# Constant products in the pauses of TensorE, split buffers by table, and an accumulator turned before the last down step

## What is computed

```python
def first_block(x, c, ctx, c_ctx, ...):                 # two layers
    for i in range(DEPTH):
        sh1, sc1, g1, sh2, sc2, g2 = ada(c, ada_w[i], ada_b[i])
        h = rmsnorm(x, norm1_g[i]) * (1 + sc1) + sh1
        out = even_mixer(h, h_ctx, ...) if i == 0 else fourier_mixer(h, w_fourier)
        x = x + g1 * out
        x = x + g2 * swiglu(rmsnorm(x, norm2_g[i]) * (1 + sc2) + sh2, w1, w3, w2)
    return x

def second_block(x, c, ...):                            # one layer
    h = rms_norm(x, g_mix) * (1 + sc1) + sh1
    x = x + gt1 * parallel_mixer(h, ...)                # window attention and RG-LRU, merged
    h = rms_norm(x, g_ffn) * (1 + sc2) + sh2
    x = x + gt2 * moe_ffn(h, ...)                       # 32 experts, 4 for a token
    return rms_norm(x, g_final)
```

## Time and profile before

| | us |
|---|---|
| median of 3 runs | 1897.08 (1891.97 to 1900.2) |
| the profiled execution | 1898.97 |
| its span | 1897.2, mean granted clock 0.941 |
| PE busy | 1692.5 (89%) |
| DVE busy | 878.2 (46%) |
| ACT busy | 441.0 (23%) |
| POOL busy | 363.7 (19%) |
| DMA | 586.61 MB, mean 309 GB/s |

### The profile page before, as it was taken

The page is one execution under the profiler, slowest core; times in us unless marked ns, Lnnn a source line. Parts: engine busy times, 40 slices in busy tenths (PEclk is TensorE's granted clock), DMA queues, the critical chain, the costliest instruction groups (busy, mean ns, idle before and its releaser), DMA issues.

```text
span 1897.2 us, 24286 instructions
## 1 busy us (share of the span) xinstructions
PE 1692.5 (89%) x9444; PEld 1071.0 (56%) x9444; DVE 878.2 (46%) x1175; ACT 441.0 (23%) x679; POOL 363.7 (19%) x119
## 2 busy tenths in 40 slices
PE   6989889999889999786899999999986989799776
PEld 2863579999589999664733444334332433344222
DVE  5767579988549988676321221221121212122012
ACT  3324544443334443454200000000000000000001
POOL 1632035553245553553000000000000000000000
PEclk8998989999999999898799999999998989899988
DMA  8623358886338877443599999999999999999994
GB/s 326 238 88 105 118 211 279 285 282 233 137 141 280 286 277 242 150 178 111 231 403 422 421 422 421 421 422 421 420 421 421 421 421 420 421 415 418 422 421 196
DMA packets 100607, 586.61 MB, mean 309 GB/s; under 512 B 12225, under 2 KB 13505, under 8 KB 45153
## 3 DMA queue, kind: packets, MB, share of 16 engines
q1 hardware_dynamic: 100512, 585.35, 79.1%
HBM read 584.26 MB, written 1.05 MB: 309 GB/s over the span
## 4 chain that ended last, share of the span: by engine, by line
PE 57%; DVE 19%; DMA 16%; issue 4%; SPq 3%; ACT 2%; DVEq 0%; ACTq 0%
PE psum L1032 21%; PE psum L1048 10%; DVE accl L1617 7%; DMA araw<-ada_dram 7%; DMA mraw<-dn_dram 4%; PE psum L611 3%; PE psum L1008 3%; PE psum L612 3%; PE psum L613 3%; SPq L398 2%; DMA mraw<-gu_dram 2%; PE psum L1061 2%; DVE accl L1616 2%; DMA mlast<-gu_dram 1%; DVE work L1672 1%
## 5 line engine op out<-in xcount | busy, mean ns | idle before, releaser
L1552 POOL TENSOR_TENSOR wl<-raw,wh 128x1024 fp32r<-128x1024 f32 (+1 forms) x100 | 353.9, 3549 | 510.5 <-ACT wh L1160 291.1
L1032 PE MATMUL psum<-mraw,xsat 128*64 128x512 f32 (+2 forms) x1648 | 413.6, 640 | 40.0 <-DMA mraw<-gu_dram 26.5
L1032 PEld LDWEIGHTS psum<-mraw,xsat 128*64 128x64 f32 (+2 forms) x1648 | 137.3, 143 | 271.5 <-issue 270.5
L1048 PE MATMUL psum<-mraw,xsat 128*64 128x512 f32 (+2 forms) x848 | 208.1, 636 | 12.7 <-DMA mraw<-dn_dram 9.9
L793 PE MATMUL psum<-ah,wh 128*128 128x256 f32 x704 | 203.8, 289 | 15.6 <-DVE al L1676 11.0
L794 PE MATMUL psum<-al,wh 128*128 128x256 f32 x704 | 201.9, 287 | 0.0
L795 PE MATMUL psum<-ah,wl 128*128 128x256 f32 x704 | 201.7, 287 | 0.0
L611 PE MATMUL psum<-ah,wh 128*128 128x256 f32 (+1 forms) x440 | 136.0, 309 | 32.6 <-DVE al L1676 9.5
L1032 PE MATMUL psum<-mlast,xsat 128*64 128x512 f32 (+2 forms) x400 | 146.3, 653 | 16.6 <-DMA mraw<-gu_dram 16.6
L793 PEld LDWEIGHTS psum<-ah,wh 128*128 128x128 f32 x704 | 137.5, 195 | 17.4 <-issue 11.5
L2190 DVE TENSOR_TENSOR oacc<-psum,oacc 128x512 f32<-128x512 f32 x60 | 38.7, 686 | 222.8 <-PE psum L1061 222.8
(11 more groups left out here) (354 smaller groups left out, 2548.0 us busy)
## 6 DMA issues: line engine op xcount, KB each, us to landing
mraw<-gu_dram SPq DMA_DIRECT2D x206, 1024.0 KB, 20.2
mraw<-dn_dram SPq DMA_DIRECT2D x106, 1024.0 KB, 25.5
araw<-ada_dram SPq DMA_DIRECT2D x128, 512.0 KB, 4.5
mlast<-gu_dram SPq DMA_DIRECT2D x50, 1024.0 KB, 21.4
raw<-ffa_dram SPq DMA_DIRECT2D x44, 1024.0 KB, 7.4
raw<-blk_dram SPq DMA_DIRECT2D x56, 512.0 KB, 3.4
raw<-ffb_dram SPq DMA_DIRECT2D x44, 512.0 KB, 5.6
mlast<-dn_dram SPq DMA_DIRECT2D x22, 1024.0 KB, 26.4
```

What stands on the lines that cost most here:

```text
L1032: last = mm(ps[4 + n][a * w:(a + 1) * w, :], xs[:, k * P + a * w:k * P + (a + 1) * w], slots[slot][:, i * 2 * D + n * 512:i * 2 * D + (n + ...
L1048: last = mm(ps[n][a * w:(a + 1) * w, :], at[:, k * P + a * w:k * P + (a + 1) * w], slots[slot][:, i * D + n * 512:i * D + (n + 1) * 512], ...
L1552: sub = lambda o, a, b: nc.gpsimd.tensor_tensor(o, a, b.bitcast(F32), ALU.subtract)
```

## The change

`keep_clock(n)` makes n constant fp32 products (ones by a constant) into bank 7, at six places: 4 behind the sums of norm 1 and the ada columns, 4 behind the loop columns of norm 2, 7 behind the sums of norm 3, 5 behind the loop columns of norm 4, 12 in front of the wait for the merged activations, 7 behind the sums of norm 5. The split buffer of a block comes from a table (`SPLIT`), and the raw blocks 21 to 36 lie behind the first feed-forward slots (`RAW`), so that those can be loaded while blocks are still running. SP issues blocks 21 to 25 and the first feed-forward loads (`ffn_first`) ahead of `ada` 28 to 47; two of the next three blocks are loaded at the end of `ffn`, and the third (the "shared" one, 27 or 36) behind six `ada` chunks and the last `b` split. ACT splits the first feed-forward slots around the last two blocks of a mixer (`last_blocks`), and the next stage's first three blocks at the end of `ffn`, ahead of the squares of norms 2 and 4. POOL does the same in its order, and three times waits for activations before it goes on with blocks (`s_h`, `s_hl`, `s_mnl`). In the tail `sum_turn()`, the 16 transposes of `oacc`, stands ahead of the last chunk of the last down step, and the output tiles lie in five banks in place of eight.

```diff
@@ -44,7 +44,10 @@
 NB = 56
-NRAW, NSPLIT = 3, 6
+NRAW = 3
+SPLIT = [b % 6 for b in range(B_O)] + [0, 1, 4, 5, 2, 3, 4, 5] * 2 + [0, 1, 4, 5, 2, 3] * 2 + [0, 1] + [4, 3, 5, 2, 0, 1, 5, 2]
+SPLIT_BEFORE = [max([k + 1 for k in range(b) if SPLIT[k] == SPLIT[b]], default=0) for b in range(NB)]
+RAW = [(5120 if B_O + NRAW <= b < B_2 + NRAW else 0) + (b % NRAW) * D for b in range(NB)]
...
@@ -345,8 +348,7 @@
         def out_tile(j):
-            bank = (3, 4, 5, 6, 7, 2, 0, 1)[j]
-            return ps[bank][:, 0:T]
+            return ps[(4, 5, 6, 7, 2)[j % 5]][:, (j // 5) * T:(j // 5 + 1) * T]
...
@@ -387,7 +389,7 @@
                     sp.wait_ge(s_lo, b - NRAW + 1)
-                sp.dma_start(raw[:, (b % NRAW) * D:(b % NRAW + 1) * D], blk_d[b]).then_inc(s_raw[b % NRAW], 16)
+                sp.dma_start(raw[:, RAW[b]:RAW[b] + D], blk_d[b]).then_inc(s_raw[b % NRAW], 16)
...
@@ -425,15 +427,11 @@
             ada(25)
-            for b in range(B_O + NRAW, B_O + NSPLIT):
-                blk(b)
...
             ada(27)
-            for b in range(B_O + NSPLIT, B_F):
+            sp.wait_ge(s_v, 4)
+            for b in range(B_O + NRAW, B_F):
                 blk(b)
-            for n in range(28, 48):
-                ada(n)
...
@@ -441,13 +439,21 @@
+            def ffn_first(l):
+                if l == 0:
+                    sp.wait_ge(s_lo, B_O + 2)
+                else:
+                    sp.wait_ge(s_flo, NF)
+                    sp.wait_ge(s_fblo, NF)
+                ffn_a(l, 0, ffna_d[l, 0])
+                ffn_b(l, 0, ffnb_d[l, 0])
+                if l == 0:
+                    sp.wait_ge(s_lo, B_O + NRAW)
+                ffn_a(l, 1, ffna_d[l, 1])
             def ffn(l):
-                sp.wait_ge(s_lo, B_F if l == 0 else B_2)
-                if l == 0:
-                    sp.wait_ge(s_v, 4)
-                for f in range(2):
-                    ffn_a(l, f, ffna_d[l, f])
-                    ffn_b(l, f, ffnb_d[l, f])
+                sp.wait_ge(s_lo, B_F - 1 if l == 0 else B_2)
+                ffn_b(l, 1, ffnb_d[l, 1])
...
@@ -464,24 +470,32 @@
                         ffn_b(l, u % 2, ffnb_d[l, bass.ds(f, 1), :, :].rearrange("a p n -> p (a n)"))
+                shared = B_F + 1 if l == 0 else B_2 + 2
+                for b in range(shared - 1, shared + 2) if l == 0 else range(B_2, B_2 + NRAW):
+                    if b != shared:
+                        blk(b)
...
                     ada(base_n + 40 + j)
+                sp.wait_ge(s_fblo, (l + 1) * NF)
+                blk(shared)
...
                     sp.dma_start(tabs[:, :, :, :], tab_d).then_inc(s_par, 16)
-                else:
-                    sp.wait_ge(s_flo, 2 * NF)
-                    sp.wait_ge(s_fblo, 2 * NF)
-                    for b in range(B_2, B_2 + NRAW):
-                        blk(b)
...
+            ffn_first(0)
+            for n in range(28, 48):
+                ada(n)
             ffn(0)
-            for b in range(B_F, B_2):
+            for b in range(B_F + NRAW, B_2 - 2):
+                blk(b)
+            ffn_first(1)
+            for b in range(B_2 - 2, B_2):
...
             ffn(1)
+            sp.wait_ge(s_flo, 2 * NF)
...
@@ -506,7 +520,7 @@
                 expert_load(i)
-            sp.wait_ge(s_blk, NB - 3)
+            sp.wait_ge(s_blk, NB - 6)
...
@@ -599,10 +613,14 @@
+            def keep_clock(n):
+                for _ in range(n):
+                    mm(ps[7][:, 0:T], ones, con[:, 0:T], start=True, stop=True)
...
                 wait(pe, s_ev, b - 1)
-                w0 = (b % NSPLIT) * D
+                w0 = SPLIT[b] * D
...
@@ -820,12 +838,14 @@
             ada_columns(5)
+            keep_clock(4)
...
             loop_columns(0)
+            keep_clock(4)
...
@@ -851,12 +871,14 @@
             norm_sums(3)
+            keep_clock(7)
...
             loop_columns(1)
+            keep_clock(5)
...
@@ -931,12 +953,14 @@
                 last.then_inc(s_msum, 1)
+            keep_clock(12)
...
             norm_sums(5)
+            keep_clock(7)
...
@@ -988,6 +1012,12 @@
+            def sum_turn():
+                for j in range(DJ):
+                    for t in range(TT):
+                        mm(out_tile(j)[:, t * P:(t + 1) * P], oacc[:, t, j * P:(j + 1) * P], ident,
+                           start=(j < 5 and t == 0), stop=False, is_transpose=True, skip_group_check=True)
...
@@ -1113,6 +1143,11 @@
                                 slots_turn(u + 1)
+                            if c == DN_CH - 1 and u == NU and p_ == 0:
+                                pe.wait_ge(m["added"], 2 * (NU - 1))
+                                pe.wait_ge(m["at"], 2 * NU)
+                                pe.wait_ge(m["gu_read"], 2 * NU)
+                                sum_turn()
...
@@ -1128,17 +1163,13 @@
                 pe.wait_ge(s_pick, PASSES + 1)
+                sum_turn()
...
-            pe.wait_ge(m["added"], 2 * (NU - 1))
-            pe.wait_ge(m["at"], 2 * NU)
+            pe.wait_ge(s_last, 2)
             for j in range(DJ):
-                if j == 6:
-                    pe.wait_ge(s_last, 2)
-                for t in range(TT):
-                    mm(out_tile(j)[:, t * P:(t + 1) * P], oacc[:, t, j * P:(j + 1) * P], ident, start=(t == 0), stop=False,
-                       is_transpose=True, skip_group_check=True)
-            for j in range(DJ):
+                if j >= 5:
+                    pe.wait_ge(s_x, 2 * DJ + j - 4)
...
@@ -1156,9 +1187,8 @@
                 act.wait_ge(s_raw[b % NRAW], 16 * (b // NRAW + 1))
-                wait(act, s_blk, b - NSPLIT + 1)
-                A(wh[:, (b % NSPLIT) * D:(b % NSPLIT + 1) * D], raw[:, (b % NRAW) * D:(b % NRAW + 1) * D], ACT.Copy
-                  ).then_inc(s_hi, 1)
+                wait(act, s_blk, SPLIT_BEFORE[b])
+                A(wh[:, SPLIT[b] * D:(SPLIT[b] + 1) * D], raw[:, RAW[b]:RAW[b] + D], ACT.Copy).then_inc(s_hi, 1)
...
@@ -1169,8 +1199,6 @@
                     A(work[:, j, 0:T], x[:, j, :], ACT.Square).then_inc(s_sq, 1)
-                    if n == 3 and j == 5:
-                        ffn_hi(1, 0, 16)
...
@@ -1265,7 +1293,7 @@
                 v_copy(t)
-            for b in range(B_O + NRAW, B_O + NSPLIT):
+            for b in range(B_O + NRAW, B_F - 2):
...
@@ -1298,19 +1326,27 @@
             A(ah3[:, 3, 0:T], ps[1][:, 0:T], ACT.Copy).then_inc(s_ao, 1)
-            for b in range(B_O + NSPLIT, B_F):
-                block_hi(b)
-            def x_by_blocks(b):
-                return lambda j: act.wait_ge(s_ev, b + j + 1)
-            def x_by_ffn(k):
-                return lambda j: act.wait_ge(s_x, DJ * k + j + 1)
...
+            def last_blocks(l, end):
+                act.wait_ge(s_blk, end - 6)
+                ffn_hi(l, 0, 16)
+                block_hi(end - 2)
+                block_hi(end - 1)
+                act.wait_ge(s_blk, end - 2)
+                ffn_hi(l, 1, 16)
+            last_blocks(0, B_F)
+            def x_by_blocks(b):
+                return lambda j: act.wait_ge(s_ev, b + j + 1)
+            def x_by_ffn(k):
+                return lambda j: act.wait_ge(s_x, DJ * k + j + 1)
...
@@ -1341,13 +1377,17 @@
                         down_hi(NF - 1, (NF - 1) % 2, 16 * ((NF - 1) // 2 + 1))
+                next_block = B_F if l == 0 else B_2
+                act.wait_ge(s_fgu, (l + 1) * NF - 1)
+                block_hi(next_block)
+                block_hi(next_block + 1)
+                act.wait_ge(s_fdn, (l + 1) * NF)
+                block_hi(next_block + 2)
...
             act.wait_ge(s_blk, B_F)
-            ffn_hi(0, 0, 16)
             h_hi(1, 3)
-            ffn_hi(0, 1, 16)
...
@@ -1355,7 +1395,7 @@
             act.wait_ge(s_fdn, 1 + NF)
-            for b in range(B_F, B_F + NRAW):
+            for b in range(B_F + NRAW, B_2 - 2):
...
@@ -1363,15 +1403,11 @@
                 A(ah3[:, c, 0:T], ps[c % 2][:, 0:T], ACT.Copy).then_inc(s_f2h, 1)
-                if c in (2, 4, 6):
-                    block_hi(B_F + NRAW + c // 2 - 1)
-            for b in range(B_F + NSPLIT, B_2):
-                block_hi(b)
+            last_blocks(1, B_2)
...
             h_hi(3, 9)
-            ffn_hi(1, 1, 16)
...
@@ -1379,17 +1415,14 @@
             act.wait_ge(s_fdn, 1 + 2 * NF)
-            block_hi(B_2)
             norm_root(4)
-            for b in range(B_2 + 1, B_2 + NRAW):
-                block_hi(b)
             h_hi(4, 12)
-            for b in range(B_2 + NRAW, B_2 + NSPLIT):
+            for b in range(B_2 + NRAW, B_2 + 6):
...
             A(lam[:, 1, :], lam[:, 0, :], ACT.Exp, scale=-1.0).then_inc(s_lru, 1)
-            for b in range(B_2 + NSPLIT, B_XG):
+            for b in range(B_2 + 6, B_XG):
...
@@ -1554,28 +1587,39 @@
                 pool.wait_ge(s_hi, b + 1)
-                s = slice((b % NSPLIT) * D, (b % NSPLIT + 1) * D)
-                sub(wl[:, s], raw[:, (b % NRAW) * D:(b % NRAW + 1) * D], wh[:, s]).then_inc(s_lo, 1)
```

(35 more changed lines are left out.)

10 lines of the change are left out of this document (5 added, 5 removed).

## The result

Over six runs each the changed kernel takes 1907.39 us (1904.99 to 1911.51) and the kernel before 1897.45 us (1891.97 to 1902.16): ratio 1.005, 95% interval 1.0033 to 1.0068. The change makes the kernel slower by 10 us, where 8 us of gain were forecast, and lies 2.4 us outside the range. The profiled execution took 1905.24 us, 6.3 over the profiled one of before; the other 3.7 us of the difference of medians are where the two profiled executions stand in their own spread (2.2 under one median, 1.5 over the other).

The account below looks back on a forecast made before the run. Expert weight streaming was taken to bound about 948 to 1873 us, so only gains before the first expert product or after the last landing count; terms summed to 8.2 us of gain, forecast 1890 us, range 1876 to 1905.

Parts of the forecast that it names:

- A0: Attention: ada loads queued behind block 25 and feed-forward loads make DVE wait 6.2 us more; -5.0 us (a loss).
- A: Norm 1: earlier POOL work frees L1672 and a pause, but holds two DVE accumulations; +0.9 us gained.
- B: Norm 2: squares start late, then Fourier products run at full clock without a second pause; -1 us (a loss).
- D: Norm 4: squares 7.0 us late, against a hold-up, a pause and a cold stretch removed; +1 us gained.
- C: Norm 3: the pause for wl and its cold stretch go, less 1.3 us; +2.4 us gained.
- E: Merge: three scans freed from POOL's splits, and half the cold block products' cost gained; +3.9 us.
- F: Norm 5, router: L953's 32 small products take about 4.7 us at full clock, not 7.01; +2.3 us gained.
- G: Tail: transposes moved into the pause keep the clock up for the last chunk; +3.7 us gained (0.8 to 4.9).
- Rival 2: Loads at ada 28 and the shared blocks of norms 2 and 4 land later; slower, 1905 to 1910; chance 0.12.
- Rival 4: Constant products leave the clock low behind the pauses; B, D, E, F lose 1.5 us each; 1895; chance 0.10.
- Rival 3: Tail: the transposes do not hold the clock, the last chunk stays at 0.50; 1893; chance 0.10.

Follow-up runs that it names:

- e12: Kernel before with 47 more constant products in its untaken branch, so nothing executed changes; 1900.88 us, ratio 1.0013.
- e2: Changed kernel with ACT converting blocks 27, 28 and 36 behind the root of norms 2 and 4, not ahead of the squares; 1898.8 us, ratio 0.9995.
- e1: Changed kernel with ada chunks 28 to 35 issued ahead of the first feed-forward loads; 1909.65 us, ratio 1.0057.
- e7: Changed kernel with the three first feed-forward loads issued in SP's idle time, ahead of the wait for the attention's values; 1904.57 us, ratio 1.0024.
- e3: Changed kernel with the tail of the kernel before (16 transposes behind the branch, eight banks); 1907.72 us, ratio 1.0041.
- e9: Kernel before with POOL's two splits of the first feed-forward slots held until DVE has scaled norm 1's chunks; 1907.27 us in one execution.
- e6: Kernel before with the constant products alone, at the same six places and in the same numbers; 1893.8 us, ratio 0.9967.
- e5: Changed kernel without its constant products at any of the six places; 1910.11 us, ratio 1.0048.
- e10: Changed kernel with the edits of e7, e2 and e4, and POOL splitting blocks 27 and 28 only after norm 2's chunks are scaled; 1895.64 us, ratio 0.998.
- e4: Changed kernel with eight more constant products in the untaken branch, so nothing executed changes; 1903.51 us, ratio 1.0028.
- e8: Changed kernel with the edits of e7, e2 and e4 together; 1890.14 us, ratio 0.9956.
- e11: Kernel before plus constant products, accumulator transposes ahead of the last chunk, longer untaken branch, and POOL waits ahead of blocks 52 and 26; 1889.45 us, ratio 0.9951.

## Why the prediction was wrong

In the profiled pair the change loses 6.3 us where the sum had 8.2 of gain, 14.5 apart. By the table 5.8 of this are the tail, 3.5 norm 3, 3.3 norm 4, 2.1 the attention and 1.6 norm 2. Two steps failed in a way that further runs bear out: the tail had no term for PE standing still while code is loaded, and the shared block was taken to be issued ahead of the end of the feed-forward layer, not behind it.

**The order on SP's queue (A0)** was right in mechanism and nearly in size: 5.50 us of wait against 6.2. The 1.2 that I had DVE make up was not made up; a second wait of 0.97 and a third of 0.59 followed instead. From 176 to 240 us DVE waits 9.0 us for `ada` chunks, and 2.1 before: -7.1 for -5.0.

**Norm 1 (A)** was right in mechanism: L1672 at 1.28, no wait on `wl`, the accumulations held in their new place. Four of them were held, not two (15.3 us for 5.1), and the sums took 5.2 us for 3.6, at clock 1.00, because the last two squares waited for DVE. Even so the change had gained 0.4 us at the start of ffn 0 and 1.9 more at its end: +2.3. That this is so near to +0.9 is in part luck, since e12 moves by 3.4 in this stage with no change at all.

**Norms 2 and 4 (B, D).** The step that failed here is the issue time of the shared block. I took 473.88, 0.5 us ahead of the end of the feed-forward layer; it was 481.19, 1.5 us behind that end (at norm 4 it was 772.66, 1.6 behind). The cause is in the rows: POOL's split of block 26, which the change puts there, holds two accumulations (4.62 us for 2.67 before), and SP's `ada` loads, which stand ahead of the shared block, wait for these. Without the hold the issue would have come 2 us earlier, by these rows; no run moves POOL's split alone, so this part is read and not tested. I had seen the hold of DVE by POOL at norm 1 and not followed it into SP's queue. The landing itself took 5.0 us, I had 5.4. So the squares were late by 9.4 at norm 2, against the end of the layer, and not by 7.9. PE's sums ended 9.0 us late, I had 7.0, and of this the Fourier products gave back 6.4 (30.3 us to block 26 for 36.6; e12 took 32.8), I had 6.2. What the late squares cost is shown by e2, which took both away and gained 10.5 us. At norm 4 the sums end 7.7 us late; behind them, up to block 34, the change gains 6.4 us where I had 7.8 (hold-up, second pause, cold stretch), and the stage from there to the merge ran 1 us longer. But that stage took 91.4 us before and 98.9 in e12, so the sign of D is not shown, nor is its size.

**Norm 3 (C)** came out with the wrong sign. The pause for `wl` went, but what is next was mis-sized: PE then waits for DVE's `ml` in ffn 1, in total 13.2 us in 14 waits, 3.1 at most, where it was 8.7 in 13 with 1.3 at most:

```profile
PE psum L806 <- DVE ml L1899: 8.7, 13, 1.3
```

```profile
PE psum L824 <- DVE ml L1946: 13.2, 14, 3.1
572.45 4.62 DVE L1946 TENSOR_TENSOR ml<-mm_,mh 128x256 fp32r<-128x256 f32 x1 [0.56 <-ACT mh L1358]
```

The second row is `ml` held by POOL's operation of 572.19 to 576.8. I had put 1.3 us on this; it was 4.5. But these waits of PE for `ml` are 7.3 us in e1, 8.9 in e7 and 11.9 in e3, whose code in ffn 1 is that of the changed kernel, and 8.4 in e12; ffn 1 as a whole took 205.9 us in e1 and 211.5 in e3 (208.3 before, 209.4 here). So the gain of 2.4 did not come, and whether there is a loss is open.

**The merge (E)**: the four scans are short (2.44 us together for 5.78), and 3.4 us are gained up to block 48. But these 3.4 us stand in e12, e9 and e6 as well, which leave POOL's order here as it was. There POOL's splits began just ahead of another, short operation of DVE (at 868.10 and 868.28 us in e12) and held that one, and PE waited 5.5 us for it:

```profile
868.28 4.66 DVE L2027 TENSOR_SCALAR p<-p,wcol 128x256 f32<-128x256 f32 x2
878.22 2.44 DVE L2067 TENSOR_TENSOR_SCAN acc<-work 128x256 f32<-128x256 f32 x4
```

So the long scans were one of the places where POOL and DVE can meet, seen in one execution, and my row for E was not typical; what the wait of POOL is worth is not shown. The block products behind were 0.9 us longer and not shorter: the clock was 0.50 from 897.0 to 900.4 in spite of 12 constant products, as in e6. The half I took for the clock was nothing here; in e2, with the same constant products and 3.75 us of pause behind them (3.26 here), the clock stayed at 1.00 and the blocks took 24.1 us for 25.6. **The router (F)** gained twice what I took, 4.6 us: L977 takes 3.98 us at clock 1.00, and the products behind, for which I had put nothing, 3.09 and not 3.65. From norm 5's sums to the first expert product it is 24.3 to 25.9 us in the ten traces with constant products and 27.2 to 29.0 in the four without, so this gain is real and lies between 1.3 and 4.7.

**The tail (G)** was the largest miss, 3.7 forecast and -2.1 measured. The clock's part came as forecast: the last chunk took 3.64 us in the profiled execution. The step that failed is that I let the final products follow at once: they stood still for 3.02 us, and 15 of them then took 5.64 us at a clock of 0.59 where all 16 had taken 3.62. I had no term for a load of code, and the page of before does show that such loads exist (59 packets on the queue for instructions). The lower end of G was 0.8, a gain, and no row excluded a loss.

**The rivals.** Rival 2 (late landings) had the right sign and named the right three places, with the wrong reason at the two norms: the landings were on time (5.0 us at norm 2), the issues weren't. Its price of 1905 to 1910 holds the result, but a third of the loss is the tail, which it does not have. Rival 4 is wrong for the whole, since e6 shows the constant products to work, and right at the merge of this execution. Rival 3: with the transposes in front, the last chunk took 3.64 us in five runs (changed, e1, e2, e5, e10), where PE's pause behind the transposes was 1.5 to 2.1 us, and 5.1 to 5.3 in four (e4, e7, e8, e11), where it was 2.8 to 3.1. Without them it took 5.2 to 6.5 us behind pauses of 3.6 to 4.9. The nearest pair is the profiled one: the chunk ahead had taken 6.30 us before and 6.39 in the changed kernel, and from its end to the last chunk it was 3.6 and 3.5 us; without transposes in it the last chunk ran at 0.50 in the main, with them at 1.00 throughout. The Trainium skill ("TensorE: Matmul & The Clock Gate", "Part 4: PE-mode transpose") says that a transpose doesn't count as PE being busy in the same way; by that rule the last chunk of the five should have been as cold as that of the kernel before, and these rows do not agree. But pauses of different length stand behind the two groups, and the chunk ahead was slow in the five (5.9 to 6.5 us) and faster in the four (4.9 to 5.2), so this stays unsettled. In sum I put 12% on slower. What the forecast lacked was this: SP, ACT and POOL had each got new work ahead of what other engines wait for, and I did not follow one queue's delay into the next.

## What to carry to other kernels

If an operation is moved to a place where its engine is idle, follow the engines that share its port, and the queue whose loads wait for them: here, by the rows, POOL's split held DVE, DVE held SP's loads, and these held ACT. A load that is brought forward belongs where its queue is idle, as in e7, not in front of a double-buffered stream. The length of code that never runs can decide microseconds behind a branch; look for "issue" in the chain of the end before a small tail edit is judged. And before a row becomes a term of a sum, see whether a second execution of the same code has it.

## What the runs showed of the hardware

Code comes in pieces of 16 KB (0.97 MB in 59 packets on the instruction queue before). PE stood still between the first and the second final product for 3.02 us (changed), 2.29 (e1), 2.21 (e7) and 2.61 (e2), and one such transfer went out within 0.4 us of the beginning of each of these standstills; in e12, where it went out 1.7 us ahead, it was 0.65 us. In e2 another 1.93 us of "issue" stand ahead of the first product. With some 32 more instructions in the branch ahead there was no standstill (e4, e8, e10), nor in e11, e3 and e5, whose code has other lengths. Behind the standstill of 2.21 us the clock was still 1.00 (15 products in 3.40 us); behind those of 2.29, 2.61 and 3.02 it was down to 0.50 for a part of them (6.22, 4.90 and 5.64 us).

DVE operations on SBUF operands that began beside a subtraction of POOL took about as long as POOL still needed, and then their own time: 5.55 us for 1.27 (norm 1, before), 3.32 for 1.23 (e9), 4.66 for 0.62 (two scalings of `p`, e12). The residual from PSUM among POOL's splits took 0.47 us, as elsewhere.

Three runs of one kernel are not enough for effects of this size: single executions of e6, an edit worth 6.3 us, ranged from 1888.18 to 1901.21.
